# First two projection tiles from tokens times norm weight, and one-off work moved into the layer

## The reference

```python
def rms_norm(x, g):
    y = xf * lax.rsqrt(jnp.mean(xf * xf, axis=-1, keepdims=True) + EPS)
    return y * g

u = rms_norm(x, lp['norm_g'])          # 1024 features
proj = u @ lp['w_in']                  # z, conv inputs, gates, latents, queries
# four head groups: Mamba-2 SSD, mLSTM, latent attention over 2048 cached
# positions, attention into 256 memory tokens, each times silu(z)
y = jnp.concatenate([ya, yb, yc, yd], axis=-1) @ lp['w_out']
return x + y                           # then the next layer, then a last rms_norm
```

## Time and profile before

| | us |
|---|---|
| median of 3 runs | 1460.26 |
| lowest and highest of them | 1458.42, 1460.96 |
| the profiled execution | 1465.72 |
| its span in the trace | 1464.0 |
| PE busy (93% of the span) | 1364.0 |
| DVE busy (41%) | 602.7 |
| ACT busy (29%) | 429.6 |
| mean granted TensorE clock | 0.954 of full speed |

### The profile page before, as it was taken

How to read it: one execution, slowest core, us unless ns; L and a number is a source line. 1 busy time by engine, 2 the same in 40 slices (tenths; PEclk the granted TensorE clock), 3 DMA queues, 4 the chain that set the end, 5 groups by cost and what they waited for, 6 DMA issues and landing times.

```text
span 1464.0 us, 23153 instructions
## 1 busy us (share of the span) xinstructions
PE 1364.0 (93%) x7072; PEld 1115.1 (76%) x7072; DVE 602.7 (41%) x1308; ACT 429.6 (29%) x1037; POOL 77.6 (5%) x132
## 2 busy tenths in 40 slices
PE   7999999799899999979979999898998999999797
PEld 5876876568788888867868867666687888888586
DVE  3042134425655555552121521343255555555611
ACT  1121233114444444430002212421153444444300
POOL 0000000000000000000000000000000000000000
PEclk9999999789999999997989999997899999999899
DMA  8543320115344544401474332201162445455032
GB/s 332 172 139 118 127 90 22 60 45 181 113 158 153 160 157 158 158 31 58 144 256 145 125 145 87 89 22 66 66 201 89 142 153 160 153 161 166 16 107 95
DMA packets 92509, 183.75 MB, mean 126 GB/s; under 512 B 15067, under 2 KB 66020, under 8 KB 80742
## 3 DMA queue, kind: packets, MB, share of 16 engines
q1 hardware_dynamic: 78710, 109.69, 22.9%
q0 software_dynamic: 9088, 64.49, 12.8%
q10 hardware_dynamic: 4608, 8.39, 1.5%
HBM read 168.63 MB, written 13.90 MB: 125 GB/s over the span
## 4 chain that ended last, share of the span: by engine, by line
PE 48%; issue 41%; POOL 3%; DMA 2%; DVE 2%; ACT 1%; POOLq 1%; DVEq 1%; SPq 0%; ACTq 0%
PE ps L473 21%; PE ps L897 8%; POOL states L435 2%; PE ps L699 2%; PE ps L657 2%; PE ps L665 2%; PE ps L482 2%; DMA par<-in_par 1%; PE ps L519 1%; DMA ring<-in_weights 1%; PE ps L770 1%; PE ps L538 1%; PE ps L499 1%; PE ps L498 1%; PE ps L507 1%
## 5 line engine op out<-in xcount | busy, mean ns | idle before, releaser
L560 PE MATMUL ps<-wk,scr 128*128 128x258 f32 x2048 | 467.7, 382 | 1.5 <-ACT scr L976 1.5
L560 PEld LDWEIGHTS ps<-wk,scr 128*128 128x128 f32 x2048 | 378.7, 190 | 52.0 <-ACT scr L976 3.2
L473 PE MATMUL ps<-uT,ring 128*128 128x264 f32 x1376 | 336.1, 405 | 16.7 <-DVE uT L1367 10.5
L473 PEld LDWEIGHTS ps<-uT,ring 128*128 128x128 f32 x1376 | 272.0, 200 | 77.9 <-issue 28.0
L1221 DVE TENSOR_REDUCE ssq<-scr 128x4 f32<-128x512 f32 x256 | 170.6, 681 | 131.0 <-ACT scr L976 129.4
L976 ACT ACTIVATE scr<-ps 128x512 f32<-128x512 f32 x256 | 151.5, 595 | 11.7 <-DVE ssq L1221 11.7
L897 PE MATMUL ps<-pt,ring 128*128 128x264 f32 x512 | 124.4, 404 | 3.9 <-DVEq L1635 3.9
L897 PEld LDWEIGHTS ps<-pt,ring 128*128 128x128 f32 x512 | 101.5, 199 | 22.8 <-issue 4.7
L973 ACT ACTIVATE raws<-ps 128x4 f32<-128x4 f32 x256 | 44.3, 173 | 222.1 <-PE ps L560 222.1
L966 ACT ACTIVATE scr<-ps 128x512 f32<-128x512 f32 x128 | 76.1, 594 | 54.1 <-PE ps L547 54.1
L547 PE MATMUL ps<-cst,lat 128*128 128x128 f32 x512 | 81.7, 282 | 4.9 <-ACT lat L1140 2.8
(11 more groups left out here) (296 smaller groups left out, 1341.2 us busy)
## 6 DMA issues: line engine op xcount, KB each, us to landing
ring<-in_weights POOLq DMA_DIRECT2D x60, 1024.0 KB, 5.0
lat<-in_lat SPq DMA_DIRECT2D x256, 128.0 KB, 2.9
rows<-rowscr SPq DMA_DIRECT2D x16, 1024.0 KB, 7.9
lat<-in_weights SPq DMA_DIRECT2D x8, 1024.0 KB, 7.4
kr<-in_krope SPq DMA_DIRECT2D x256, 32.0 KB, 2.0
uT<-in_memv SPq DMA_DIRECT2D x16, 512.0 KB, 3.6
uT<-in_memk SPq DMA_DIRECT2D x16, 512.0 KB, 5.8
states<-in_ssm SPq DMA_DIRECT2D x16, 256.0 KB, 3.3
```

The source lines that it names most:

```text
L473: last = mm(ps[:, bank, 0:T], w[:, k, :], u3[:, k, :], start=k == 0, stop=k == KT - 1)
L560: last = mm(ps[:, 1 + 2 * (j % 2) + half, 0:258], latT[:, g % 2, q, c, :], wk[:, 2 * c + half, at:at + 258], start=c == 0, stop=c == 1)
```

## The change

The head of a layer no longer waits for the root.

- DVE also keeps `xg`, the tokens times the norm weight. It lies in `xc[:, 0:8]`. DVE writes it before the loop for layer 0, and in the tail of a layer, tile by tile, for the next one. The norm weight (the first 8 columns of `par`) is therefore loaded apart and early: at the start for layer 0, and in layer 0 for layer 1.
- PE computes projection tiles 0 and 1 from `xg` (`first_tiles`). The sum of the eighth block of squares, which finishes the root, is put between the fourth and fifth matmul of tile 0. DVE multiplies the two tiles by the root as it takes them out of PSUM. Tiles 2 and later use `uT` as before, now written as `xg` times the root.
- Tiles 0 to 19 are written out on PE, and the tiles use the banks in another rotation: tile m lies in bank (m + 2) mod 4, tiles 0 and 1 in banks 2 and 3.
- The squares and the root of the memory tokens, which were done once before the loop, are now done in each layer: ACT squares them after tile 4, DVE adds the eight blocks up pairwise to one, and PE sums that one block over the partitions after tile 8. DVE's normalisation of the memory tokens moves from ahead of tile 1 to behind tile 9.
- The memory tokens are loaded once per layer and no longer once more at the start. The high constants move from the start into each layer, behind the store of the latents.

The diff, cut to its core:

```diff
@@ sync
+            for part in range(2):
+                sp.dma_start(xT[:, k, :], d["xT"][:, k, :]).then_inc(x_in[part].sem, 16)
-            sp.dma_start(cst[:, 0:K_MASK], d["cst"][:, 0:K_MASK]).then_inc(first.sem, 16)
-            sp.dma_start(memn, d["memT"]).then_inc(mem_first.sem, 16)
-            sp.dma_start(cst[:, K_MASK:], d["cst"][:, K_MASK:]).then_inc(second.sem, 16)
-            sp.dma_start(pages[:, :], d["pages"]).then_inc(second.sem, 16)
+                if part == 0:
+                    sp.dma_start(par[:, 0:C_CW], one("par", 0)[:, 0:C_CW]).then_inc(norm_in.sem, 16)
+                    sp.dma_start(cst[:, 0:K_MASK], d["cst"][:, 0:K_MASK]).then_inc(first.sem, 16)
+            sp.dma_start(pages[:, :], d["pages"]).then_inc(pages_in.sem, 16)
             with sp.Fori(0, DEPTH) as l:
                 sp.wait_ge(*layer_free(l, 0))
-                sp.dma_start(par[:, :], one("par", l)).then_inc(par_in.sem, 16)
-                sp.wait_ge(m_sq.sem, 1)
+                sp.dma_start(par[:, C_CW:], one("par", l)[:, C_CW:]).then_inc(par_in.sem, 16)
                 sp.dma_start(memn, d["memT"]).then_inc(mem_in.sem, 16)
-                sp.wait_ge(second.sem, 32)
+                sp.wait_ge(*xg_ready(l, KT))
+                sp.dma_start(par[:, 0:C_CW], one("par", DEPTH - 1)[:, 0:C_CW]).then_inc(norm_in.sem, 16)
+                sp.wait_ge(pages_in.sem, 16)
...
                              pt[:, CKV:CKV + 2, :]).then_inc(saved.sem, 16)
+                sp.dma_start(cst[:, K_MASK:], d["cst"][:, K_MASK:]).then_inc(second.sem, 16)
@@ tensor
+            def first_tiles(l):
+                w = slot(l, 0).rearrange("p (a k m) -> p a k m", a=2, k=KT)
+                for a in range(2):
+                    for k in range(KT):
+                        if a == 0 and k == 0:
+                            pe.wait_ge(*xg_ready(l, KT - 1))
+                        if a == 0 and k == KT // 2:
+                            x_sum(l - 1, KT - 1, stop=True).then_inc(x_ss.sem, 1)
+                        if a == 0 and k == KT - 1:
+                            pe.wait_ge(*xg_ready(l, KT))
+                        last = mm(ps[:, 2 + a, 0:T], w[:, a, k, :], xg[:, k, :], start=k == 0, stop=k == KT - 1)
+                    last.then_inc(pj_mm.sem, 1)
...
-            for k in range(KT):
-                pe.wait_ge(x_sq.sem, k + 1)
-                last = mm(ps[:, 4, 0:T], ones, u3[:, k, :], start=k == 0, stop=k == KT - 1)
-            last.then_inc(x_ss.sem, 1)
-
-            pe.wait_ge(m_sq.sem, 1)
-            for k in range(KT):
-                last = mm(ps[:, 5, 0:MEM], ones, pt[:, k, 0:MEM], start=k == 0, stop=k == KT - 1)
-            last.then_inc(m_ss.sem, 1)
+            for k in range(KT - 1):
+                x_sum(-1, k, start=k == 0)
             with pe.Fori(0, DEPTH) as l:
-                with pe.Fori(0, LOOPED // 4) as i:
...
+                first_tiles(l)
+                for m in range(2, 20):
+                    first_tile(m)
+                    if m == 8:
+                        pe.wait_ge(*m_add(l, 1))
+                        mm(ps[:, 5, 0:MEM], ones, memsq[:, 0, :], start=True, stop=True).then_inc(m_ss.sem, 1)
...
+                pe.wait_ge(*second(l, 16))
                 pe.wait_ge(*g_wend(l, 1))
...
-                x_sum(OUT_TILES - 2)
-                x_sum(OUT_TILES - 1, stop=True).then_inc(x_ss.sem, 1)
+                x_sum(l, OUT_TILES - 2)
                 pe.drain().then_inc(layer_free.sem, 1)
+            x_sum(DEPTH - 1, OUT_TILES - 1, stop=True).then_inc(x_ss.sem, 1)
@@ scalar
             with act.Fori(0, DEPTH) as l:
+                x_root(l)
                 act.wait_ge(*layer_free(l, 0))
...
+                tile_out(2)
+                tile_out(4)
+                act.wait_ge(*mem_in(l, 16))
+                fn(memsq, memn, ACT.Square).then_inc(m_sq.sem, 1)
+                tile_out(6)
+                tile_out(8)
+                act.wait_ge(*m_ss(l, 1))
+                root(rsm, ps[:, 5, 0:MEM], 1.0 / D_MODEL).then_inc(m_rs.sem, 1)
@@ vector
+            dve.wait_ge(norm_in.sem, 16)
+            for k in range(KT):
+                ts(xg[:, k, :], xT[:, k, :], col(C_NORM + k), None, ALU.mult).then_inc(xg_ready.sem, 1)
             with dve.Fori(0, DEPTH) as l:
-                dve.wait_ge(*layer_free(l, 0))
-                dve.wait_ge(*par_in(l, 16))
                 dve.wait_ge(*x_rs(l, 1))
                 for k in range(KT):
-                    last = stt(u3[:, k, :], xT[:, k, :], col(C_NORM + k), nrs[:, 0, :], ALU.mult, ALU.mult)
+                    last = tt(u3[:, k, :], xg[:, k, :], nrs[:, 0, :], ALU.mult)
...
+                dve.wait_ge(*layer_free(l, 0))
+                dve.wait_ge(*pj_mm(l, 2))
+                for m in range(2):
+                    last = tt(pt[:, m, :], ps[:, 2 + m, 0:T], nrs[:, 0, :], ALU.mult)
+                last.then_inc(first_out.sem, 1)
...
+                tile_out(5)
+                dve.wait_ge(*m_sq(l, 1))
+                tt(memsq[:, 0:4], memsq[:, 0:4], memsq[:, 4:8], ALU.add)
...
+                tile_out(9)
+                dve.wait_ge(*par_in(l, 16))
+                dve.wait_ge(*m_rs(l, 1))
+                for k in range(KT):
+                    last = stt(memn[:, k, :], memn[:, k, :], col(C_MEM + k), rsm, ALU.mult, ALU.mult)
+                last.then_inc(mem_ready.sem, 1)
...
                         tt(x2, x, x, ALU.mult).then_inc(x_sq.sem, 1)
+                        ts(xg[:, bass.ds(2 * i + c, 1), :].rearrange("p o t -> p (o t)"), x, par[:, bass.ds(2 * i + c, 1)], None,
+                           ALU.mult).then_inc(xg_ready.sem, 1)
```

More of the change, by code:

```diff
@@ L55 @@
 IN_CHUNKS = (IN_TILES + 1) // 2
-LOOPED = 20
 FIRST_TILES = 23
@@ L213, in build @@
         gdt, acum, wend, la, li, lf, gi, nmx, mT = (gates[:, i, :] for i in range(9))
-        first, second, mem_first = sig("first_loads"), sig("second_loads"), sig("mem_first_in")
+        first, pages_in, second = sig("first_loads"), sig("pages_in"), sig("second_loads", 16)
         x_in = [sig("x_low_in"), sig("x_high_in")]
-        layer_free = sig("layer_free", 4, 4)
+        norm_in, layer_free = sig("norm_weight_in", 16), sig("layer_free", 4, 4)
         par_in, wsm_in, mem_in = sig("par_in", 16), sig("wsm_in", 32), sig("mem_in", 16)
@@ L270, in _, with one @@
         def _(sp):
+            def one(name, i):
+                return d[name][bass.ds(i, 1)].rearrange("o p n -> p (o n)")
             for part in range(2):
```

109 lines of the change are left out of this document (51 added, 58 removed).

## The result

| | before | after |
|---|---|---|
| median of the runs | 1460.63 us (6 runs, 1458.42 to 1468.19) | 1450.18 us (6 runs, 1449.21 to 1452.05) |
| ratio after / before | | 0.9922, 95% interval 0.9896 to 0.9948 |
| profiled execution (span) | 1465.72 us (1464.0) | 1450.64 us (1448.9) |
| PE busy | 1364.0 us | 1354.2 us |

The changed kernel is faster by 10.45 us in the medians (11.4 by the ratio, 7.6 to 15.2 by its interval). The forecast was 18.6 us, 1441.7; the time lies 8.5 us above that and 2.2 us above the end of the range. The direction was right, the size was not.

The account below looks back on a forecast made before the run. PE's work was taken as the bound (busy 1364.0 of 1464.0 us). Gains 10.0 + 11.0 less 1.2, 0.9 and 0.3 make 18.6, so 1460.26 becomes 1441.7 us; likeliest range 1438.5 to 1445, 8-in-10 to 1448.

Parts of the forecast that it names:

- The seam: Between the layers, last output tile to end of tile 1: tile 1 ends at 742.5 instead of 753.56, gain 11.0 us.
- rival B: At the jump back to the layer's head, a pause of 3 us plus 2.4 of low clock: 1447.1 us; chance 9%.
- The start: Layer 0 up to tile 1's end: tile 0 at 11.6, tile 1 done at 19.2 instead of 29.18, gain 10.0 us.
- The ring at tile 4: Layer 1: tile 4 waits 1.2 us for its ring slot beside SP's loads, a cost; bounds 0 and 3.3.
- Memory tokens: In each layer, one sum of 256 columns on PE costs 0.45 us, 0.9 in all; the rest costs 0.
- High constants: Loaded in each layer behind the store of the latents; SP waits for nothing new: 0, ends 0 and 0.5 us.
- Tiles written out: 18 projection tiles stand in the code once each instead of four in a loop, with other banks: cost 0.
- End: Last sum stands behind the drain and the exit from the loop: cost 0.3 us, ends 0 and 1.
- Rival A: Ring becomes the bound at start and seam, PE meeting SP's loads: gain only 13.1, 1447.2 us; chance 16%.
- C: Rival: nothing is gained, because the time comes back downstream of the moved memory norm and constants: 1460; chance 2%.
- D: Rival: slower, as written-out tiles 2 to 19 each pay a PE pause; at 0.6 us a tile 1463; chance 2%.

## Why the prediction was wrong

**The seam, 11.0 us, failed on one step: "I add 0.3 us for the drain and take 734.9 for tile 0".** The drain and the jump back were 5.06 us, 4.8 more than the 0.3, and tiles 0 and 1 took 9.93 us at the low clock, 2.4 more than the 7.56 written (7.64 where the jump was gone). These are the 7 us that are missing. The mechanism was on paper as rival B, with the right place and the right second part. It got 9% because of one argument: that PE jumps back in the sample loop with no gap. That loop has no drain ahead of its jump, and its body is shorter; without the drain the long jump has no gap either. An argument from a row counts only where the row has all the parts of what it stands for. B as priced (3 us and 2.4) would have given 1447.1; the gap was 5 and the start was short besides.

**The start, 10.0 us, failed on "that half lands where the constants did, near 6.9, with at most one us more".** It landed at 12.93. The place in SP's queue was read as the time of landing. But in the kernel before, the constants had the third place and landed at 6.87, and in the changed one they still have it, and landed at 8.70; the tokens' half moved from the second place to the fourth. The load in the fourth place is the one that runs beside the whole 2 MB of the slots. The same code landed it at 10.8 to 13.8 in seven traces, so this is no chance of one run. The prediction had the price before its eyes, the 13.93 us of `par`, put it down to the two large loads in its queue, and did not ask who else was on the engines. All else in that step was near: the norm weight's products took 0.28 us each within the bounds of 0.18 and 0.42, eight squares and sums as forecast, and from tile 0's start to tile 1's end 7.67 us where 7.6 was written. The low end of this term, 6.2, did not hold it either (5.2).

**The ring at tile 4, 1.2 us: 0.18 was measured**, because PE came 5 us late and at the low clock, so that SP's loads had mostly landed. Where the pause was taken away the term was mis-sized the other way: 3.43, 3.61 and 3.69 us, which is the 3.3 that the prediction wrote as its upper bound. The load took 10.1 us where the jump was gone, not the 7.6 of equal shares. The Trainium skill, page "DMA: Bandwidth & Descriptors", section "Queues, rings and completion order", has each DMA engine take turns between the queues, a packet at a time. From equal turns the prediction had worked out a wait of 1.2 us at tile 4, and three traces show about three times that; why the ring got less than an equal share is open.

**Memory tokens, 0.9 us: right.** The sum's two rows are in each layer, the square took 1.90 us (2.1 forecast) and the additions 1.22, 0.69 and 0.43, all beside PE's work:

```profile
49.38 0.59 PE L660 MATMUL ps<-lat,cst 128*128 128x256 f32 x2
...
753.72 1.90 ACT L1050 ACTIVATE lat<-lat 128x2048 f32<-128x2048 f32 x1
...
757.34 1.22 DVE L1414 TENSOR_TENSOR lat<-lat 128x1024 f32<-128x1024 f32 x1
```

**High constants, 0: right**; issued at 109.50, landed 6.4 us later, and nothing waited. **Tiles written out, 0: right**, 32 rows in 7.28 us. **End, 0.3: 0**; from the start of the last sum to the end of the span it is 9.4 us in both.

The sum as it was: 5.2 + 4.0 - 0.9 (memory) - 0.9 (ring waits 6.3 in all, against 5.4) = 7.4 us by the trace, against 10.45 in the medians and an interval of 7.6 to 15.2. The 3 us between are not explained place by place. At equal granted clock the times differ by about 8 us, so most of it is stretches of low clock, which come and go between executions. By that reading the 10.45 flatter the change a little. Rival A's place was right and its moment wrong: the ring did become a bound, but only in the kernels where the pause was gone. C and D did not come about. By the trace the gain is 11.2 us short of the forecast (7.4 of 18.6), by the medians 8.2; the difference was not foreseen by any term, it is mostly clock, and so luck.

## What to carry to other kernels

When a wait of several microseconds is taken away, list what stands at the same place beneath it: here a jump behind a drain (5 us) and then a weight load behind other loads (3.5 us), each of which only shows when the one above it is gone. Before the time of a single run is believed, its mean granted clock is to be compared: 0.004 of it were some 6 us here. Where a kernel is like this one, a drain directly ahead of a long loop's jump back is to be avoided; let the last instruction signal instead. And in this kernel a transfer that an engine waited for came in time only when it had the DMA engines nearly to itself: hold back, or put half-way between two of them, the transfers that nobody needs yet; a repair that moves company to another place must be read at that place too.

## What the runs showed of the hardware that was not expected

- Drain and jump back together 5.0 to 5.5 us on PE, in every kernel that had both; drain alone 0.23 (two kernels), jump alone 0 (four kernels).
- A load of 4 KB issued fourth took 9 to 11 us beside 2 MB of GpSimd's loads, and 3.6 us issued second.
- PE's wait of 3.69 us at tile 4 was followed by a granted clock of 0.50; one of 3.43 us at the same tile, in the kernel without the drain, by 1.00.
- A store of 66 KB in 1536 pieces of 44 bytes took 13.7 us, and a 1 MB load issued meanwhile took 9.9 us (the next one 5.0), so that PE waited 3.3; moved, it made 1.4 MB of constants take 14.7 us instead of 6.4.
- The landing of the low constants, by one and the same code and order, varied from 5.03 to 9.99 us between runs. The start of tile 0 varied with the loads there, from 14.19 to 17.14 us in seven traces. What a first load costs is not to be read from one execution.
